# Seven half-size products for k, values and output gates in the first mixer of a two-block model kernel

## The reference, cut to what matters

```python
u = rmsnorm(x, norm_g) @ w_in            # 1024 x (512 q, 512 k, 1024 v, 1024 o, 4 + 4 gates)
q, k, v, o, gi, gf = jnp.split(u, M_SPLITS, axis=-1)
i_pre, f_pre = gi + b_gates[0], gf + b_gates[1]
h = mlstm_chunkwise(q * M_DQK ** -0.5, k, v, i_pre, f_pre)    # 4 heads, causal, with running maximum
h = rmsnorm(h, h_norm_g)
h = h * jax.nn.sigmoid(o)
return h @ w_out
```

## Time and profile before

| | us |
|---|---|
| median of 3 runs | 993.83 (993.49 to 993.85) |
| profiled execution, its own time | 993.23 |
| its span, first to last instruction | 991.4 |
| TensorE busy | 977.4 (99%) |
| VectorE busy | 632.2 (64%) |
| ScalarE busy | 270.2 (27%) |

### The profile page before, as it was taken

The page is one execution under the profiler, slowest core; times in us unless marked ns, Lnnn a source line. Parts: engine busy times, 40 slices in busy tenths (PEclk is TensorE's granted clock), DMA queues, the critical chain, the costliest instruction groups (busy, mean ns, idle before and its releaser), DMA issues.

```text
span 991.4 us, 15109 instructions
## 1 busy us (share of the span) xinstructions
PE 977.4 (99%) x5783; PEld 875.8 (88%) x5783; DVE 632.2 (64%) x1399; ACT 270.2 (27%) x588; POOL 1.1 (0%) x8
## 2 busy tenths in 40 slices
PE   7999999999999999999999999999999999999997
PEld 6887889999999988888899999999888878888876
DVE  2402637788688571244377876885699972699963
ACT  0212212211211122145122112111443354634461
POOL 0000000000000000000000000000000000000000
PEclk9999999999999999999999999999999999999999
DMA  9991045777677192460527766771853412533201
GB/s 279 349 355 59 1 148 170 262 254 248 213 255 269 68 335 89 133 207 1 161 90 270 260 229 228 250 268 59 265 173 128 139 64 60 191 127 126 64 1 43
DMA packets 133060, 170.81 MB, mean 172 GB/s; under 512 B 8707, under 2 KB 120595, under 8 KB 132883
## 3 DMA queue, kind: packets, MB, share of 16 engines
q1 hardware_dynamic: 128560, 167.79, 51.5%
q10 hardware_dynamic: 4451, 2.35, 0.9%
HBM read 168.93 MB, written 2.64 MB: 173 GB/s over the span
## 4 chain that ended last, share of the span: by engine, by line
PE 90%; DVE 8%; ACT 1%; DMA 1%; issue 1%; ACTq 0%; DVEq 0%
PE bank L1145 25%; PE bank L1158 15%; PE bank L919 12%; PE bank L930 10%; PE bank L1426 5%; DVE work L2004 4%; PE bank L1121 3%; PE bank L1413 2%; PE bank L1319 2%; PE bank L1338 2%; PE bank L1069 1%; PE bank L1267 1%; PE bank L970 1%; PE bank L1285 1%; PE bank L1361 1%; PE bank L1090 1%
## 5 line engine op out<-in xcount | busy, mean ns | idle before, releaser
L1158 PE MATMUL bank<-work,fring 128*128 128x256 f32 x704 | 155.6, 379 | 0.0
L1158 PEld LDWEIGHTS bank<-work,fring 128*128 128x128 f32 x704 | 132.1, 190 | 17.0
L1839 DVE SCALAR_TENSOR_TENSOR work<-work,cols 128x256 f32<-128x256 f32 x176 | 71.6, 479 | 53.2 <-ACT work L637 53.2
L2004 DVE SCALAR_TENSOR_TENSOR work<-work,cols 128x256 f32<-128x256 f32 x240 | 98.7, 478 | 1.6 <-ACT work L790 1.1
L1145 PE MATMUL bank<-sq,fring 128*128 128x128 f32 x640 | 84.5, 275 | 0.0
L637 ACT ACTIVATE work<-work,cols 128x256 f32<-128x256 f32 x88 | 45.6, 589 | 122.1 <-DVE work L1818 100.8
L1145 PE MATMUL bank<-sq,ring 128*128 128x128 f32 x640 | 78.0, 275 | 0.0
L1145 PE MATMUL bank<-ring,fring 128*128 128x128 f32 x640 | 78.0, 275 | 0.0
L1145 PEld LDWEIGHTS bank<-sq,fring 128*128 128x128 f32 x640 | 77.9, 192 | 0.0
L919 PE MATMUL bank<-xg,ring 128*128 128x256 f32 x352 | 77.5, 380 | 0.0
L1145 PEld LDWEIGHTS bank<-ring,fring 128*128 128x128 f32 x640 | 76.2, 192 | 1.0
(11 more groups left out here) (300 smaller groups left out, 1315.8 us busy)
## 6 DMA issues: line engine op xcount, KB each, us to landing
fring<-in_f_w_up SPq DMA_DIRECT2D x44, 1024.0 KB, 7.5
work<-in_w_ada SPq DMA_DIRECT2D x32, 768.0 KB, 6.2
fring<-in_f_w_down SPq DMA_DIRECT2D x22, 1024.0 KB, 5.0
ring<-in_w_in SPq DMA_DIRECT2D x18, 1024.0 KB, 5.3
ring<-in_a_w_in SPq DMA_DIRECT2D x11, 1024.0 KB, 12.1
ring<-in_w_kv SPq DMA_DIRECT2D x8, 1024.0 KB, 5.4
ring<-in_w_out SPq DMA_DIRECT2D x8, 1024.0 KB, 5.1
ring<-in_a_w_out SPq DMA_DIRECT2D x4, 1024.0 KB, 12.1
```

The source lines that it names most:

```text
L1158: last = mm(pb[m // 2][:, T * (m % 2):T * (m % 2 + 1)], w[:, k, P * m:P * (m + 1)], f_act[:, par, T * k:T * (k + 1)], start=(first and k = ...
L1839: ins = v.scalar_tensor_tensor(f_t[q][:, c, :], f_u[:, q, c, tap:tap + T], col(f"f_conv_w{f}", 44 * tap + n), f_t[q][:, c, :], ALU.mult, A ...
L2004: marks[c] = link(v.scalar_tensor_tensor(b_y[:, c, :], b_a[:, c, tap:tap + T], col("conv_w_2", 124 * l + 4 * tap + c), b_y[:, c, :], ALU.m ...
```

## The change

Slots 2 to 11 are taken as five pairs (k: 2, 3; values: 4, 5 and 6, 7; output gates: 8, 9 and 10, 11). Each pair becomes seven half-size products as in the feed-forward: k and the output gates by features (`by_features`, 128 columns), the values by tokens (`by_tokens`, 256 columns). VectorE makes the four weight sums of each pair (`m_sums_of`) and the x differences `m_t`, and puts the results together (`halves_out`, `v_out`) in SBUF before they are scaled; ScalarE copies the first product of each. The sums lie in parts of `fring` that the feed-forward's first loads used to fill, so those loads go behind product 11. The four output gate halves now all stand behind the last head, and the heads' scores and numerators in one run ahead of them; before, slots 8 and 9 were multiplied between the heads. The gate columns alternate between output partitions 0 to 63 and 64 to 127, and VectorE adds the two. At the start x comes in four quarters on ScalarE's queue and slot 0 in four quarters on SyncE's, slot 0's steps stand between the turns of x, `hT` is copied by ScalarE, ahead of its parameter DMAs, and four idle products on ones are added at the very front. PSUM banks are dealt anew. The diff, cut:

```diff
+        M_PAIRS = ((2, 3), (4, 5), (6, 7), (8, 9), (10, 11))
+        K_BANK = ((2, 3), (4, 5))
+        V_BANK = ((6, 4, 5, 0), (6, 2, 3, 7))
+        O_HALF_BANK = ((0, 1), (7, 4))
...
-            for m in (1, 3):
-                sp.dma_start(x_rows[:, :, 256 * m:256 * m + 256], x_quarter(m)).then_inc(S(f"x_in{m}"), 16)
+            sp.dma_start(a_norm_rows, I["a_norm"].rearrange("l (c p) -> (l c) p", p=P)).then_inc(S("a_in"), 16)
             first_w = cut(I["a_w_in"][0], 0)
-            sp.dma_start(slot8(0)[:, 0:4, :], first_w[:, 0:4, :]).then_inc(S("first_half"), 16)
-            sp.dma_start(slot8(0)[:, 4:8, :], first_w[:, 4:8, :]).then_inc(S("ring0"), 16)
+            for m, sem in enumerate(("first_w", "x_in1", "x_in2", "ring0")):
...
+                sp.dma_start(slot8(0)[:, 2 * m:2 * m + 2, :], first_w[:, 2 * m:2 * m + 2, :]).then_inc(S(sem), 16)
...
+            load_up(0, 0, 0, True)
+            for n in range(8, 16):
+                load(n)
+            product(sp, 11)
+            load_up(0, 1, 1, True)
...
-            act.dma_start(x_rows[:, :, 0:256], x_quarter(0)).then_inc(S("x_in0"), 16)
-            act.dma_start(a_norm_rows, I["a_norm"].rearrange("l (c p) -> (l c) p", p=P)).then_inc(S("a_in"), 16)
-            act.dma_start(x_rows[:, :, 512:768], x_quarter(2)).then_inc(S("x_in2"), 16)
             for m in range(4):
-                act.wait_ge(S(f"x_in{m}"), 16)
+                act.dma_start(x_rows[:, :, 256 * m:256 * m + 256], x_quarter(m)).then_inc(S(f"x_in{m}"), 16)
+            tables(LN_EXP)
+            for m in range(4):
+                act.wait_ge(S("xg_ready"), 2 * m + 2)
+                nc.scalar.activation(hT[:, 2 * m:2 * m + 2, :], three(pb[X_BANK[m]][:, :], 2), ACT.Copy)\
+                    .then_inc(S("h_ready"), 1)
...
             squares(0)
+            def first_out(u, dst, bank):
+                act.wait_ge(S("three_done"), u + 1)
+                nc.scalar.activation(dst, bank, ACT.Copy).then_inc(S("p1_out"), 1)
+            for c in range(2):
+                first_out(c, W(K_RAW[c] + 512, K_RAW[c] + 640), pb[K_BANK[c][0]][:, 0:P])
...
+            def v_scaled(p):
+                act.wait_ge(S("m_raw"), 3 + p)
+                act.wait_ge(S("rcol_done"), 1)
+                raw = W(V_RAW, V_RAW + 1024).rearrange("p (j b n) -> p j b n", j=2, b=TB)
+                for b in range(TB):
+                    nc.scalar.activation(three(m_v[:, b, 512 * p:512 * p + 512], 2), raw[:, :, b, :],
+                                         ACT.Copy, scale=rcol[:, b:b + 1]).then_inc(S("m_v_out"), 1)
...
+            v_scaled(0)
+            v_first_out(1)
+            for h in range(4):
+                decay(h)
+            v_scaled(1)
+            act.wait_ge(S("m_v_out"), 4)
...
+            turn_x(0)
+            pe.wait_ge(S("first_w"), 16)
+            for k in range(DC):
+                if k in (1, 3, 5):
+                    turn_x(k // 2 + 1)
+                if k == 6:
+                    pe.wait_ge(S("ring0"), 16)
+                pe.wait_ge(S("xg_ready"), k + 1)
+                for c in range(2):
+                    last = mm(pb[0][:, T * c:T * (c + 1)], slot8(0)[:, k, P * c:P * (c + 1)], xg[:, k, :],
+                              start=(k == 0 and c == 0), stop=(k == DC - 1), skip_group_check=True)
+            last.then_inc(S("product"), 1)
...
+            def factors(p, i):
+                val, gate = [slot8(n) for n in M_PAIRS[p]]
+                return ((val[:, 0:4], x11), (val[:, 4:8], x21), (m_s2[p % 2], m_t[1]), (m_s1[p % 2], m_t[0]),
+                        (gate[:, 0:4], m_t[2]), (m_sl[p % 2], x22), (gate[:, 4:8], m_t[3]))[i]
+            def by_features(p, c, banks, which):
+                for i in which:
+                    w, x = factors(p, i)
+                    dst = pb[banks[0]][:, P * i:P * i + P] if i < 3 else pb[banks[1]][:, P * (i - 3):P * (i - 2)]
+                    for k in range(4):
+                        last = mm(dst, w[:, k, P * c:P * (c + 1)], x[:, k, :], start=(k == 0), stop=(k == 3))
+                return last
...
+            def by_tokens(p, i, dst):
+                w, x = factors(p, i)
+                for k in range(4):
+                    last = mm(dst, x[:, k, :], w[:, k, :], start=(k == 0), stop=(k == 3))
...
+            arrived(pe, 2)
+            for c in range(2):
+                by_features(0, c, K_BANK[c], (0, 1))
+            sums_ready(0)
+            for c in range(2):
+                by_features(0, c, K_BANK[c], (2,)).then_inc(S("three_done"), 1)
+                last = by_features(0, c, K_BANK[c], (3, 4, 5, 6))
+                if c == 0:
+                    last.then_inc(S("seven_done"), 1)
+                else:
+                    last.then_inc(S("product"), 2)
...
             pe.wait_ge(S("cols_done"), 2)
-            ss(1, pb[5][:, 0:T])
-            pe.wait_ge(S("const_in"), 32)
-            mm(pb[6][0:8, 0:3 * P], sml[0:BUCKETS, 161:169], pc("bucket", 3 * P)[0:BUCKETS, :],
-               start=True, stop=True).then_inc(S("rowsT_done"), 1)
             pe.wait_ge(S("gw_in"), 64)
...
-                last = mm(pb[4][0:64, 0:T], m_gw[:, k, :], xg[:, k, :], start=(k == 0), stop=(k == DC - 1))
+                o = 64 * (k % 2)
+                last = mm(pb[7][o:o + 64, T:2 * T], m_gw[:, k, :], xg[:, k, :], start=(k < 2), stop=(k >= DC - 2),
+                          skip_group_check=True)
             last.then_inc(S("m_gate_proj"), 1)
+            ss(1, pb[7][:, 0:T])
...
+            arrived(pe, 4)
+            first, second, third, fourth = [pb[i] for i in V_BANK[0]]
+            by_tokens(1, 0, first[:, half[0]])
+            pe.wait_ge(S("m_raw"), 2)
+            by_tokens(1, 1, second[:, half[0]])
+            sums_ready(1)
+            by_tokens(1, 2, second[:, half[1]]).then_inc(S("three_done"), 1)
+            by_tokens(1, 3, third[:, half[0]])
...
+            arrived(pe, 6)
+            first, second, third, fourth = [pb[i] for i in V_BANK[1]]
+            pe.wait_ge(S("p1_out"), 3)
+            by_tokens(2, 0, first[:, half[1]])
+            pe.wait_ge(S("rcol_done"), 1)
+            by_tokens(2, 1, second[:, half[0]])
+            sums_ready(2)
+            by_tokens(2, 2, second[:, half[1]]).then_inc(S("three_done"), 1)
+            pe.wait_ge(S("rows_done"), 1)
+            by_tokens(2, 3, third[:, half[0]])
...
+            for h in range(M_HEADS):
+                spread(h, SPREAD_BANK, rows[0:4, 6, :], "m_spread")
+            pe.wait_ge(S("m_k_out"), 2)
             m_scores(0)
             m_scores(1)
+            by_tokens(2, 6, fourth[:, half[1]]).then_inc(S("product"), 2)
+            m_scores(2)
+            m_scores(3)
...
+            def gate_half(u):
+                p, c = 3 + u // 2, u % 2
+                if u == 1:
+                    pe.wait_ge(S("m_num_out"), 2)
+                if u >= 2:
+                    pe.wait_ge(S("m_raw"), 3 + u)
+                if c == 0:
+                    arrived(pe, M_PAIRS[p][0])
+                by_features(p, c, O_HALF_BANK[c], (0, 1))
+                sums_ready(p)
+                by_features(p, c, O_HALF_BANK[c], (2,)).then_inc(S("three_done"), 1)
+                if u == 0:
+                    m_square_sum(3)
+                last = by_features(p, c, O_HALF_BANK[c], (3, 4, 5, 6))
+                if c == 0:
+                    last.then_inc(S("seven_done"), 1)
+                else:
+                    last.then_inc(S("product"), 2)
+            gate_half(0)
+            gate_half(1)
+            gate_half(2)
             pe.wait_ge(S("rstd_done"), 2)
-            for h in range(4):
-                spread(h, rows[0:4, 7, :], "f_spread")
-            gate_product(3, 1, range(4, DC)).then_inc(S("product"), 1)
             pe.wait_ge(S("m_num_out"), 8)
+            for h in range(M_HEADS):
+                spread(h, F_BANK, rows[0:4, 7, :], "f_spread")
+            gate_half(3)
...
+            def m_sums_of(p):
+                val, gate = [slot8(n) for n in M_PAIRS[p]]
+                for n in M_PAIRS[p]:
+                    arrived(dve, n)
+                if p >= 2:
+                    product(dve, M_PAIRS[p - 2][1])
+                s1, s2, sl = m_s1[p % 2], m_s2[p % 2], m_sl[p % 2]
+                n = link(v.tensor_tensor(s1, gate[:, 0:4], gate[:, 4:8], ALU.add))
+                v.tensor_tensor(gate[:, 0:4], val[:, 0:4], gate[:, 0:4], ALU.subtract)
+                after(n)
+                n = link(v.tensor_tensor(s2, s1, val[:, 0:4], ALU.subtract))
+                after(n)
+                v.tensor_tensor(sl, val[:, 4:8], s2, ALU.subtract).then_inc(S("s_ready"), 1)
...
+            def halves_out(u, at, banks, all_done):
+                one, two = pb[banks[0]], pb[banks[1]]
+                p1, u2, u43 = W(at + 512, at + 640), W(at + 640, at + 768), three(W(at + 768, at + 1024), 2)
+                dve.wait_ge(S("p1_out"), u + 1)
```

(100 more changed lines are left out.)

239 lines of the change are left out of this document (115 added, 124 removed).

## The result

The changed kernel takes 996.31 us (median of 8, 995.8 to 997.27) against 993.66 (median of 8, 992.77 to 995.41): ratio 1.0025, 95% interval 1.0016 to 1.0034. It is 0.25% slower; the forecast was 995.9. The end that I followed, slot 12's product, comes at 127.26 instead of 124.82; the forecast had 127.0. Behind it nothing is lost: from there to the end of the span are 866.6 us in both kernels (spans 993.9 and 991.4). But two terms of the forecast were off by some 2 us each, one either way.

What follows compares the result with a forecast made beforehand. TensorE was taken to bound the first 135 us almost alone. Terms -7.4 -2.0 +3.3 +0.8 +6.9 +0.6 were summed to +2.2 us; 993.83 + 2.1 gave 995.9 us, range 992.4 to 998.8.

Steps and rivals of the forecast that it cites:

- Half-size products: Five slot pairs, seven half-size products each: three pairs save 4.0 us, two save 3.4, together -7.4.
- Start: Slot 0's k-steps between the turns of x, in quarters: slot 0 ends at 15.9, gain -2.0 us.
- ScalarE's issuing: Parameter DMAs at the start, issued 7.4 us later, take 19.3 us (bounds 17 and 20); ScalarE free at 34.2.
- rival 1: Blocked parameter issues fall away, ScalarE free near 28: 991.9 or 991.2 us; chance 0.15.
- the wait for cols: TensorE, after pair (2, 3) and the parameter turns, waits from 36.0 to 39.3: stall +3.3 us.
- m_raw 2: VectorE's sums for pair (4, 5) ready at 46.6, TensorE there at 45.8: stall +0.8 us, +2.6 with packed gates.
- Gate columns: 16 passes alternating between column halves: gain 0 to 1.8 us, taken as 0 since TensorE waits behind them for VectorE.
- VectorE's block: Work from m_raw 2 to the first square sum takes VectorE 39.8 us, TensorE arrives at 32.9: stall +6.9 us.
- From the square sum to the end: Last heads, output gate halves and slot 12's last passes, from 39.8 to 80.6 after m_raw 2.
- Rival 3: VectorE's decay, sum and value steps overlap better, so the 6.9 becomes 4 to 5: 993 to 994 us; chance 0.10.
- rival 2: Loads later still, ScalarE's stretch 21.5 us, slot 5 at 43: 998.7 us; chance 0.15.
- Slots 12 to 15 and the feed-forward behind them: Behind slot 12's product, these loads and the late feed-forward sums were forecast to cost nothing.

Runs made afterwards that it cites:

- woven: Changed kernel with early parameter DMAs and VectorE's sum steps interleaved with value results, probabilities and squares: 986.58 us, 0.9941 to the kernel before.
- the last two edits: Against the woven kernel: six parameter turns ahead of pair (2, 3)'s last 32 passes, and three products on ones behind quarter 0's turns; 984.01 us.
- early parameters: Against the changed kernel: VectorE copies x to hT, and ScalarE begins its parameter DMAs when x has landed; 993.95 us.
- the old start: Start of the kernel before (x on both queues, slot 0 in halves, all turns first): in the changed kernel 994.21 us, in the woven one 986.71.
- unfilled quarters: Kernels with the quarter start but without the three added products on ones behind quarter 0's turns; with these the woven kernel took 985.21 us.

## Why the prediction was right, step by step

The direction, the size and the place of the largest wait were right. Of the steps:

- **Half-size products**, -7.4: nearly right. Pair (2, 3) takes 12.5 us for 112 passes, value products 1.73 for eight passes, both as forecast. The four output gate halves take 25.6 (2.88, 16.27 and 6.45 in the chain above), some 0.5 more than the forecast had for them. With the new waits mostly taken away (woven) the kernel is 6.4 under the one before, and 9.0 with the last two edits.
- **Start**: slot 0's last passes end at 17.2,

```profile
14.39 2.80 PE L1028 MATMUL bank<-xg,ring 128*128 128x256 f32 x12
```

  where the forecast had 15.9: a gain of 0.7 and not 2.0, a little outside its own bound of -1. Weights and x were later than even shares gave. The turns of quarter 1 began at 9.05 and not at 7.1; that turns took less than forecast in the chain (0.44 for the four of a quarter, in two of the three quarters, where 0.9 stood) gave part of it back. From 3.5 to 6 us the queues had

```profile
q10 hardware_dynamic: 426, 0.41, 53.3%
q1 hardware_dynamic: 328, 0.32, 40.4%
```

  against 65 to 35 with x on both the earlier trace rows. That is nearer to even, and agrees with the taking of turns by packets in the Trainium skill (DMA: Bandwidth & Descriptors, Queues, rings and completion order).
- **ScalarE's issuing**, taken at 19.3, measured 16.3 (15.5 to 31.85). This is the term that was mis-sized. One issue blocked, for 3.35, and not two for 2.48 and 4.54: part of rival 1. It is not the later hour that shortens it: begun at 10.7, with early parameters, it takes 16.1, and with the old start 19.5. So ScalarE was free 2.3 earlier than forecast, the wait for cols was 0.96 and not 3.3, and m_raw 2 came at 44.67, not 46.6. The load of tables took 1.28 and the squares followed at 33.15, as in the earlier trace rows. The 2.66 of the Trainium skill (ScalarE: Activation LUTs, What ACT_TABLE_LOAD costs) is for a switch to another set. This load was none: the changed kernel loads the same set at 2.82 already, so its second load seems to spend 1.28 of the chain for nothing (leaving that one out was not tried). But at a real switch, 103.23, the next ACTIVATE followed at 104.53 as well.
- **Gate columns**: 1.95 for 16 passes, the upper bound of the gain. That is what the Trainium skill says of column halves (TensorEngine Tiling (Array Packing), Performance Considerations). Worth next to nothing in this kernel, as taken; the wait behind it was 1.21, forecast 2.6 with packed gates, for ScalarE came earlier.
- **VectorE's block**: from m_raw 2 to the first square sum 39.3, forecast 39.8. TensorE's wait 5.4, forecast 6.9: the rest is that TensorE itself arrived 1.1 later, held by the stretch at 1.2 GHz from 68.5 to 72.
- **From the square sum to the end**: 43.3 (84.0 to 127.26), forecast 40.6. Of the 2.7, 2.4 are the five microseconds at half clock, which the prediction had at nothing: it had priced a wait only by its own length. The rest is in the output gate halves. This and the 2 of ScalarE's issuing cancel, and 995.9 came out close for that reason: the number was in part luck. (The working also ends at 80.6 and goes on with 80.4, and adds 2.1 where the sum says 2.2; neither matters here.)

Rival 3 was wrong in its mechanism (nothing overlapped better until the order was changed), rival 2 did not occur. Slots 12 to 15 and the feed-forward behind them cost nothing, as said.

## What to carry to other kernels

When work is taken from the engine that bounds a kernel and given to one with idle time, ask in which order the second engine has it queued: here some 7 us of saved passes were lost, for the most part to some 9 us of sums standing ahead of short steps that TensorE waited for. Weaving the same instructions in another order, with either repair of the start, put the kernel 6.3 to 6.4 under the one before. Price a wait of TensorE by its length and by the half clock that may follow it (2.4 us here). A small DMA list on an engine that also computes is part of the chain as soon as it starts late.

## What was not expected of the hardware

- The granted clock fell to 0.5 of full (1.2 GHz) while TensorE was idle for 5.4 us and stayed there for some 5 us of work (84 to 89); 22 passes on ones in the gap kept it at full. It also fell early in slot 0, behind idle times of 1.4 to 2.3 us, in four of the eight profiled executions with the unfilled quarters, and not behind 0.8 to 1.6 in the other four. And it fell with TensorE at work, behind the spreads (68.5 to 72.0 in the changed kernel), in four of the twelve changed kernels and not in the kernel before. What decides in those cases is open.
- The issue of a tiny DMA behind 1 MB of constants and two of 16-byte pieces was blocked for 4.54 us before the change and for 3.35 after it. It goes with the form of the start, and not with the hour: 4.3 in both kernels with the old start, 3.1 to 3.4 in all with quarters, whether issued at 21 or at 27. Which part of the start it is (x on the other queue, or what is outstanding there) was not tried.
